# Weight transfers of 4 MB with 32 KB rows in a streamed mixture of experts, one Trainium2 core

## What is computed

```
gate_a, gate_b = ...                       # (256, 1024) each
mixed = sigmoid(gate_a) * (y_a @ moba_up) + sigmoid(gate_b) * (y_b @ hgrn_up)
x = x + mixed @ w_out
h2 = rmsnorm(x, norm2_w)
top_v, top_e = top_k(h2 @ router_w + router_b, 4);  top_w = softmax(top_v)
for each expert e:                         # 1024 x 2048 and 1024 x 1024 floats: 12 MB
    gu = h2[its tokens] @ w_gate_up[e] + b_gate_up[e]
    y = ((clip(up) + 1) * glu(gate)) @ w_down[e] + b_down[e]
x = x + sum of y * top_w;  out = rmsnorm(x, final_norm_w)
```

## Time and profile before

| | |
|---|---|
| time, median of 3 runs | 1134.95 us (1134.37 to 1135.22) |
| the profiled execution's own time | 1136.25 us |
| its span, first to last instruction | 1134.5 us |
| PE busy | 1059.2 us, 93% |
| DVE, ACT, POOL busy | 348.4, 222.7, 38.9 us |
| hardware queue of SP (q1) | 436.71 MB, 92.6% of 16 engines' span |
| TensorE clock granted | 0.999 |

### The profile page before, as it was taken

How to read it: one execution, slowest core, us unless ns; L and a number is a source line. 1 busy time by engine, 2 the same in 40 slices (tenths; PEclk the granted TensorE clock), 3 DMA queues, 4 the chain that set the end, 5 groups by cost and what they waited for, 6 DMA issues and landing times.

```text
span 1134.5 us, 13360 instructions
## 1 busy us (share of the span) xinstructions
PE 1059.2 (93%) x5613; PEld 519.9 (46%) x5613; DVE 348.4 (31%) x686; ACT 222.7 (20%) x354; POOL 38.9 (3%) x32
## 2 busy tenths in 40 slices
PE   7999999999999999999988888888888898899896
PEld 7889999734343443434333333333333334233332
DVE  4984788422303222222222222222112020303022
ACT  6645674201010101011010010101010101010002
POOL 0390000000000000000000000000000000000000
PEclk9999999999999999999999999999999999999999
DMA  9545669999999999999999999999999999999994
GB/s 320 190 150 215 231 215 365 368 415 415 430 428 428 426 430 427 428 428 427 429 426 428 427 428 428 428 429 426 429 428 428 428 426 428 428 427 427 428 425 201
DMA packets 47489, 439.17 MB, mean 387 GB/s; under 512 B 5388, under 2 KB 7848, under 8 KB 22600
## 3 DMA queue, kind: packets, MB, share of 16 engines
q1 hardware_dynamic: 45136, 436.71, 92.6%
q10 hardware_dynamic: 2296, 1.61, 0.5%
HBM read 437.26 MB, written 1.05 MB: 386 GB/s over the span
## 4 chain that ended last, share of the span: by engine, by line
PE 57%; DMA 41%; DVE 1%; issue 0%; ACT 0%; another core or an unknown queue 0%; DVEq 0%
DMA S<-in_w_gate_up_dram 21%; PE PS L1671 20%; DMA S<-in_w_down_dram 12%; PE PS L1730 9%; PE PS L1338 9%; DMA B<-in_w_gate_up_dram 4%; PE PS L1652 4%; DMA EXTRA<-in_w_gate_up_dram 4%; PE PS L1632 3%; PE PS L1351 1%; PE PS L1354 1%; PE PS L1357 1%; PE PS L1712 1%; PE PS L1692 1%; PE PS L1318 1%; PE PS L1389 1%
## 5 line engine op out<-in xcount | busy, mean ns | idle before, releaser
L1671 PE MATMUL PS<-S,M 128*64 128x512 f32 x1520 | 340.0, 596 | 28.5 <-DMA S<-in_w_gate_up_dram 22.0
L1671 PEld LDWEIGHTS PS<-S,M 128*64 128x64 f32 x1520 | 105.3, 137 | 241.9 <-issue 195.7
L1171 DVE TENSOR_SCALAR M<-PS 128x256 f32<-128x256 f32 x64 | 27.0, 423 | 531.8 <-PE PS L1671 531.8
L1730 PE MATMUL PS<-S,M 128*64 128x512 f32 x736 | 164.7, 595 | 17.1 <-DMA S<-in_w_down_dram 17.1
L765 ACT ACTIVATE M<-M 128x256 f32<-128x256 f32 x64 | 26.7, 417 | 495.4 <-DVE M L1171 495.4
L1730 PEld LDWEIGHTS PS<-S,M 128*64 128x64 f32 x736 | 52.0, 137 | 119.8 <-issue 102.5
L770 ACT COPY M<-PS 64x512 f32<-64x512 f32 x31 | 17.9, 578 | 276.4 <-PE PS L1730 276.4
L1185 DVE COPY M<-PS 128x512 f32<-128x512 f32 x32 | 22.1, 692 | 127.7 <-PE PS L1712 127.7
L1632 PE MATMUL PS<-M,X 128*128 128x128 f32 x480 | 59.0, 281 | 0.0
L1632 PEld LDWEIGHTS PS<-M,X 128*128 128x128 f32 x480 | 57.7, 196 | 0.0
L1652 PE MATMUL PS<-M,SELT 128*128 128x512 f32 x120 | 55.5, 605 | 0.0
(11 more groups left out here) (259 smaller groups left out, 978.3 us busy)
## 6 DMA issues: line engine op xcount, KB each, us to landing
S<-in_w_gate_up_dram SPq DMA_DIRECT2D x95, 2048.0 KB, 47.8
S<-in_w_down_dram SPq DMA_DIRECT2D x43, 2048.0 KB, 47.2
M<-in_w_gate_up_dram SPq DMA_DIRECT2D x12, 2048.0 KB, 46.5
EXTRA<-in_w_gate_up_dram SPq DMA_DIRECT2D x11, 2048.0 KB, 48.7
S<-in_w_in_dram SPq DMA_DIRECT2D x10, 2048.0 KB, 7.9
B<-in_w_gate_up_dram SPq DMA_DIRECT2D x10, 2048.0 KB, 48.5
B<-in_w_down_dram SPq DMA_DIRECT2D x7, 2048.0 KB, 48.2
EXTRA<-in_w_down_dram SPq DMA_DIRECT2D x6, 2048.0 KB, 48.0
```

Source lines behind the costliest of these rows:

```text
L1171: v.tensor_scalar(gate[:, c], g2[:, :, 0], LIMIT, None, ALU.min).then_inc(gate_ready, 1)
L1671: ins = mm(gu[half][64 * g:64 * g + 64, :], hTe[:, k, tok], gu_slot[slot][:, kk, c:c + 512], start=(k == 0), stop=(k == KD - 1))
L1730: ins = mm(dst[64 * n:64 * n + 64, :], actT[b][:, k, 64 * kh:64 * kh + 64], dn_slot[slot][:, k, 512 * n:512 * n + 512], start=(kh == 0 and ...
```

## The change

The rows of a transfer double. `wgu` has four input channels on a partition, `wdn` eight, so that a partition's share of a quarter of gate/up, or of a whole down matrix, is 32 KB in one piece. From the second pair on, two slices are one transfer of 4 MB (`load_unit`), issued when both slots are free. The exceptions are the whole first pair, the last pair's down weights, and the unit whose two slots would be slot 9 and slot 10, which do not touch (`by_slots`); these are 2 MB transfers of 16 KB rows as before. Over the run 80 transfers of 4 MB stand for 160 of 2 MB, and 32 slices stay as they were.

The 11 slots become one tensor W. For that the early buffers move: slot 0 holds a new buffer hi_d until late, and slice 0 of the first pair is now issued after hu3 and not before group "mu"; slices 8 and 9 take the early places of 9 and 10, and 10 that of 8.

The other order of channels asks for more. POOL regroups x within its rows (`regroup`), the router's weights are loaded in that order, the residual is added through a strided view, and `act_T` turns eight groups of 64 by 16 small matmuls in place of four transposes. The gates ga, gb and the units mu, hu are made by `split`, tokens by channels, and the mix is turned back by four units mT0 to mT3 of four 128x128 transposes each, which DVE and ACT split into mix_lo and mix_hi.

```diff
-        wgu = A["w_gate_up"].rearrange("l e (s p k) n -> (l e) s p (k n)", p=P, k=2)
-        wdn = A["w_down"].rearrange("l e (h p c) n -> (l e) h p (c n)", p=P, c=4)
+        wgu = A["w_gate_up"].rearrange("l e (u p k) n -> (l e) u p (k n)", p=P, k=4)
+        wdn = A["w_down"].rearrange("l e (p c) n -> (l e) p (c n)", p=P)
...
+        def by_slots(j, m, first_round):
+
+            return not first_round or ring(j, m) == 9 or j == 0 or j == PAIRS - 1 and m >= 8
...
             for n, what in enumerate(LOADS):
                 if what == GB1:
-                    load(0, 0, 9)
-                if what == "mu":
-                    filled(sp, "kT1")
-                    load(0, 0, 0)
+                    load(0, 0, 8)
                 if what == "wo0":
                     filled(sp, "ya1")
                     load(0, 0, 1)
                 if what == "wo1":
-                    load(0, 0, 10)
+                    sp.wait_ge(x_regrouped, 1)
+                    load(0, 0, 9)
                     sp.wait_ge(yb_ready, 1)
                     load(0, 0, 3)
...
             filled(sp, "hu3")
+            load(0, 0, 0)
             load(0, 0, 5)
-            sp.wait_ge(mix_ready, 1)
-            load(0, 0, 8)
+            filled(sp, "mT3")
+            load(0, 0, 10)
             filled(sp, "wo10")
...
-            def load_pair(p, e, j, stop=12):
-
-                for m in range(stop):
-                    used(p + (m - SLOTS) // 12, (m - SLOTS) % 12)
-                    load(e, j, m)
+            def load_pair(p, e, j, first_round, stop=12):
+
+                for m in range(0, stop, 2):
+                    if by_slots(j, m, first_round):
+                        for n in (m, m + 1):
+                            used(p + (n - SLOTS) // 12, (n - SLOTS) % 12)
+                            load(e, j, n)
+                    else:
+                        for n in (m, m + 1):
+                            used(p + (n - SLOTS) // 12, (n - SLOTS) % 12)
+                        load_unit(e, j, m)
...
+            pool.wait_ge(at_ready, 1)
+            pool.wait_ge(xn_ready, TT)
+            st.did(regroup(x_spare, X[:, 0, :]))
+            st.settle()
+            st.did(regroup(rows_of(1), X[:, 1, :]))
+            st.settle()
+            nc.gpsimd.tensor_copy(rows_of(0), x_spare).then_inc(x_regrouped, 1)
...
-                for c in range(4):
-                    ins = tr((gu[1] if b else multi)[:, P * c:P * c + P], act[:, P * c:P * c + P], ident)
+                if not isinstance(i, int):
+                    tr((gu[1] if b else multi)[:, 0:P], act[:, 0:P], ident)
+                for c in range(8):
+                    for g in range(2):
+                        rows, cols = slice(64 * g, 64 * g + 64), slice(64 * c, 64 * c + 64)
+                        ins = mm((gu[1] if b else multi)[rows, cols], act[rows, cols], ident[rows, rows],
+                                 start=True, stop=True)
                 ins.then_inc(actT_filled, 1)
...
-            split_T(*GATES[9])
+            split(*GATES[9])
             wait_drained(pe, "ya1")
+            def up(name, what, j, x_hi, x_lo, lo_there):
+                split(f"{name}{j}", what, j % 2, x_hi, x_lo, lo_there, kn=4, half=j // 2)
+
+            def turn_mix(j):
+
+                ps = begin(f"mT{j}")
+                pe.wait_ge(mix_step, j + 1)
+                for a in range(4):
+                    c = unit_cols(j).start + P * a
+                    ins = tr(ps[:, P * a:P * a + P], ga[:, c:c + P], ident)
+                end(ins)
```

More of the change, by code:

```diff
@@ L92 @@
             "pos0": 5, "pos1": 2, "all": 7, "wT": 6}
+OWN_BANK.update({"hu0": 2, "hu1": 3, "mT0": 4, "hu2": 5, "mT1": 2, "hu3": 3, "mT2": 6, "mT3": 7})
 UNITS = bank_units()
@@ L1053, in _, with mix, mixed_lo @@
                 lo("hu", j)
-            for j in range(4):
-                c = slice(512 * j, 512 * j + 512)
-                ve.wait_ge(sig_ready, 3)
+            def mix(j):
+                c = unit_cols(j)
                 filled(ve, f"hu{j}")
-                drain(f"hu{j}", v.tensor_tensor(gbT[:, c], bank(f"hu{j}")[:], gbT[:, c], ALU.mult))
-                st.settle()
-                st.did(v.tensor_tensor(flat[:, c], flat[:, c], gbT[:, c], ALU.add), mix_step)
-                if j < 2:
-                    lo("wo0", j)
-            st.settle()
-            st.did(v.tensor_scalar(SMALL[:, 609:610], eps, 1.0, None, ALU.mult), mix_ready)
+                drain(f"hu{j}", v.tensor_tensor(gb[:, c], bank(f"hu{j}")[:], gb[:, c], ALU.mult))
+                ve.wait_ge(drained_by["dve"], st.count[drained_by["dve"].name])
+                st.did(v.tensor_tensor(ga[:, c], ga[:, c], gb[:, c], ALU.add), mix_step)
+            def mixed_lo(j):
+                ve.wait_ge(mix_hi_ready, j + 1)
+                drain(f"mT{j}", v.tensor_tensor(mixed_chunk(mix_lo, j), turned_mix(j), mixed_chunk(mix_hi, j), ALU.subtract))
+            ve.wait_ge(sig_ready, 3)
+            mix(0)
+            lo("wo0", 0)
+            mix(1)
+            lo("wo0", 1)
+            mixed_lo(0)
+            mix(2)
+            mixed_lo(1)
+            mix(3)
+            mixed_lo(2)
+            mixed_lo(3)
             def residual(tt, n):
@@ L1338, in split_T, with split @@
                             ins = mm(ps[:, T * a:T * a + T], w[:, k, P * a:P * a + P], x[:, k, :],
-                                     start=(k == 0 and w is w_h and x is hi), stop=(k == kn - 1 and x is lo))
+                                     start=(k == 0 and w is w_h and x is hT_hi), stop=(k == KD - 1 and x is hT_lo))
                 end(ins)
-            def split(name, what, tt, hi=hT_hi, lo=hT_lo, lo_there=(hT_lo_ready, 1)):
+            def split(name, what, tt, hi=hT_hi, lo=hT_lo, lo_there=(hT_lo_ready, 1), kn=KD, half=0):
@@ L1348, in split @@
+                w_l = w_lo[s].rearrange("p (k n) -> p k n", k=kn)[:, :, 512 * half:512 * half + 512]
                 rows = slice(P * tt, P * tt + P)
-                pe.wait_ge(hi_ready, n + 1)
-                for k in range(KD):
-                    mm(ps[:].rearrange("p (j n) -> p j n", j=2), hi[:, k, rows], w_h[:, k], start=(k == 0), stop=False)
-                wait_lo(what, 1)
-                for k in range(KD):
-                    mm(ps[:], hi[:, k, rows], w_l[:, k, :], start=False, stop=False)
+                pe.wait_ge(hi_ready, last + 1)
@@ L1469, in _ @@
                     probs_T(h - 1)
-                split_T(*GATES[4 + h // 2])
+                split(*GATES[4 + h // 2])
             for j in range(2):
@@ L1476, in _ @@
             probs_T(7)
-            split_T(*GATES[8])
+            split(*GATES[8])
             wait_drained(pe, "pT7")
```

277 lines of the change are left out of this document (154 added, 123 removed).

## The result

The changed kernel takes **1137.89 us** in the median of 18 runs (1136.86 to 1140.78); the kernel before, on the same chips, 1135.39 (18 runs, 1134.37 to 1136.54). The ratio is **1.0024**, with a 95% interval of 1.0018 to 1.003: slower by 2.5 us. The forecast was 1133.5, with a range up to 1137.6. The profiled execution of the changed kernel took 1139.23 us with a span of 1137.4, so it is 1.3 us over its median.

The account below looks back on a forecast made before the run. The prediction took the full DMA stream plus PE's work after the last landing to bound the run. Start +1.0, transfers -4.3 and tail +1.8 gave -1.5 us, a median of 1133.5 us, range 1130.3 to 1137.6.

Parts of the forecast that it names:

- Part 1: Weight stream: 4 MB units with 32 KB rows save 54 ns each, 4.3 us over 80 units; ends 0 and 7.1 us.
- the choice of 6 ns: Weight stream: fixed DMA cost a packet, taken between nothing and the 10 ns derived from 16 KB and 2 KB rows.
- 36.8 ns "for a KB": Weight stream: size-dependent part of an engine's time for a row, from two equations on 16 KB and 2 KB rows.
- Part 2: Start of the stream, through pair 1: later slice 0 and two-slot waits make it 1.0 us later; ends -1 and +3.5.
- the holes: Opening, 210 to 230 us: DMA moved 356 and 357 GB/s; filling this would absorb 1 to 5 us of slice 0's 4.9.
- DVE and ACT lie under PE there: Opening, around the mix: DVE and ACT work stays hidden under PE, which gets 1.8 us earlier at the opening pair.
- Part 3: PE in a pair and at the end: dearer act_T hidden until the last pair; PE ends the run, 1.8 us later.
- 52.8 against 58.4: Each pair: PE time with the dearer act_T against DMA time, in us, so act_T is hidden until the last pair.
- so no clock is to be won: PE, whole run: the granted clock read 1.00, the higher of two levels, in both windows, so it could not improve.
- Rival (c): Opening, mix to pair 1: PE is late and the queue runs dry, +3.4 us, 1138.4; chance 0.12.
- (a): Weight stream: the larger row saves nothing or 3 ns, giving 1135.5 to 1137.8 us; chance 0.25.
- (b): Weight stream: the full 10 ns a packet hold, -7.1 + 2.8 = -4.3, giving 1130.7 us; chance 0.18.

Follow-up runs that it names:

- experiment 1: The changed kernel with every transfer at 2 MB, keeping the new layout, `act_T`, mix and slots: 1136.99 us, ratio 1.0012 to the kernel before.
- experiment 2: The changed kernel with pair 1 (the second pair) also in 2 MB transfers: 1135.04 us, ratio 0.9992 to the kernel before.
- experiment 7: The changed kernel with pair 1 in 2 MB transfers, each two issued one after the other when both slots are free: 1138.12 us, ratio 1.0023.
- experiment 5: The kernel before with ten more 64x64 matmuls in each `act_T`, their results overwritten: 1138.79 us, ratio 1.0025 to the kernel before.
- experiment 3: The changed kernel with the last pair wholly in 2 MB transfers: 1135.85 us, ratio 1.0 to the kernel before.
- experiment 10: The changed kernel with slices 2, 3, 6 and 7 of the last pair in 2 MB transfers: 1135.49 us.
- experiment 8: The changed kernel with slices 2 and 3 of the last pair in 2 MB transfers: 1138.65 us.
- experiment 9: The changed kernel with slices 6 and 7 of the last pair in 2 MB transfers: 1138.05 us.
- experiment 11: The changed kernel with three unused 512-column matmuls in PE's wait between slices 1 and 2 of the last pair: 1137.07 us.

## Where the prediction was right and where it failed

**The bound** was read rightly: the end is the end of the stream plus what follows. Every difference found lies in one of the three places it named: the start, the stream, the tail.

**Part 1, what a transfer costs, held.** 54 ns a unit were worked out, 58 measured by the medians and 70 by the landings, 4.3 us in all for 80 units against 4.6 (80 x 0.058) to 5.6. The choice of 6 ns in place of the 10 that the earlier trace rows gave was the right one, with luck in how near it is, since it was a choice between nothing and 10: 58 = 9 x f, eight rows and a report, makes 6.4 ns a packet (5 to 8), and 70 makes 7.8. (The 36.8 ns "for a KB" are for 1000 bytes, and of the fetches, which are 16 KB packets, four stand among the 2613 rows; neither changes the sum.) In the window from 300 to 400 us there are 1618 packets at 430 GB/s:

```profile
DMA packets 1618, 42.99 MB, mean 430 GB/s; under 512 B 176, under 2 KB 176, under 8 KB 176
```

Without the 176 small ones these are 1442 rows with 42.99 MB, which makes about 1180 of 32 KB and 260 of 16 KB (two slices of 2 MB), where the earlier trace rows had 2613 of 16 KB: a row of 32 KB isn't split. The estimate of 3.5 ns from the Trainium skill (DMA: Bandwidth & Descriptors, "Why small descriptors are slow", three cycles a packet) would make 28 ns a unit (8 x 3.5); the measurement is about twice that.

**Part 2 failed, and it is the main step that did.** It allowed 1.0 us for the start of the stream (slice 7 at 272.8, the outer end +3.5); slice 7 landed 4.7 us later than before (276.46 against 271.78), of which 2.85 us are seen in the median. Against the forecast its unit was issued 1.1 us later (261.43 for 260.3) and took 2.5 us longer to land (15.0 for 12.5). By bytes alone the forecast was 269.9 to 273.9, and experiments 1 and 2 are at 271.7: giving up the idle time for slice 0 was indeed paid for by the holes. What was wrong is the wait for two slots. I priced only the last unit of pair 1, at 12.5 us after its issue. All four issues, from the trace of the changed kernel:

```profile
L460 SPq DMA_DIRECT2D W<-in_w_gate_up_dram x4: 328/328/328, 230.6 to 261.4; - x4
...
DMA to landing us min/median/max: 12.5/14.8/15.0
```

Only the first takes 12.5, and it lands 0.5 us late, at 243.03. The next is issued at 240.78, with 2.25 us of work left in the queue; it lands at 255.41, 12.4 us after its forerunner where two slices would take 9.78. The next two come 11.0 and 10.05 us after theirs. The pauses of 0.5, 2.6, 1.2 and 0.3 us add up to nearly all of the 4.7, and of this only the 1.2 us at slice 9 (experiment 2) are made up. The forecast built on the shortest landing of 2 MB, 7.6 us, for a unit that stands behind three others with such a wait each. I had looked at the depth of the queue at one issue (10.2 us for slice 7, 4.9 of them its own transfer) and called it short, but had not asked at each issue of a unit how much was left, which was the forecast's own data: some 5.3 us of work stood ahead of slice 7, and a transfer that is issued one slice later finds a good part of that gone. Experiments 2 and 7 show the rest: same transfers, one wait or two, 1135.04 or 1138.12.

PE was also only 0.8 us earlier at the opening pair (219.96 against 220.76), not 1.8, which moved the last issue by a microsecond. The timelines show most of that: when the output projection begins, PE is 1.6 us ahead (185.18 against 186.79), with the last turning unit (0.35 us) still to come. "DVE and ACT lie under PE there" did not hold: PE waits 0.21 us for DVE before the third turning unit (184.79) and 0.41 us before the matmuls at 212.19; the kernel before shows no wait at either place.

**A term was missing:** that the longer program costs time in the stream. Part 3 called the dearer `act_T` hidden, "52.8 against 58.4", by PE's time alone. Its matmuls, 1024 where there were 128, and as many weight loads are also fetched, by the same DMA engines, and the prediction put that at nothing without a reason. Experiment 1 puts all of the change but the units at 1.4 us, and its trace has that in the stream, not in the opening or the tail; experiment 5 gets such a loss from the instructions alone, and in all three traces it is some 1.5 us for a round of eight fetches. The Trainium skill describes the fetch (Runtime: NRT & Kernel Launch, "Instruction fetch mechanics": code comes in blocks of 16 KB, and the cost of it is mostly hidden). The blocks agree with the rows, 0.61 MB in 37; that they are hidden does not hold here, where the DMA queue is the bound.

**Part 3, the tail, held, with one exception.** It said that slice 6 would be reached just when 6+7 is there, that PE and not the last landing would end the run, and that this costs 1.8 us. Experiments 3 and 10 give 2.0 and 2.4 for it, experiments 8 and 9 show that both units bind at once, and experiment 11, where the clock held, has 22.9 us from the landing of 6+7 (1102.13) to the end of the last `down`, forecast 22.7. The exception is "so no clock is to be won". There was some to be lost. Sum and rivals took PE's durations from full speed, and the new wait of 3.5 us in the last pair lets the clock fall to the lower level just where PE is the bound.

**The sum.** Forecast +1.0 - 4.3 + 1.8 = -1.5. Measured by the experiments: +2.85 (pair 1), +2.0 to 2.4 (last pair, the clock's share included), +1.4 (the longer program), -4.1 (the 71 other units): +2.2 to +2.6 against 2.5. The first two are net of the 9 units' own gain.

**The rivals.** Rival (c) ended nearest, 1138.4, and its sign in the profile appeared (a window under 420 between 230 and 300 us). That sign could not tell, though: the kernel before has such windows too, 410 from 230 to 240 and 395 from 270 to 280. And its mechanism was that PE would be late, and PE was early; the queue ran short by the way the units are issued. It had the right place and consequence and the wrong cause, and a chance of 0.12 was too small for a queue that was known to be short. Rivals (a) and (b), rows that save less or more, both fall.

## What to carry to other kernels

Ask of a larger transfer first not what it saves on the wire but how much is left in the queue at each moment when it could be issued: where the queue is short, at the start of a stream, keep the transfers small, and also before its last work, where a late landing leaves the compute engine to end the run (here 2 MB in the first two pairs and the last one, 4 MB between, 0.24% faster than before). Two late landings can hold the same end, so that undoing either alone shows nothing. And in a stage that DMA bounds, count the instructions that a change adds on an engine with time to spare, since their code comes through the same DMA engines (here 1.5 us for each eight fetches of 16 KB).

## What the runs showed of the hardware that was not expected

- TensorE's clock fell to its lower level (1.2 GHz) after PE had stood still for 3.5 us in the last pair, and sixteen matmuls took 5.35 and 6.53 us in two traces, 3.65 at full speed. In experiment 8 it fell after 2.65 us (5.17 us), in experiment 1 after 2.04 (5.35 us). It held after 2.04 us in the kernel before, 2.17 in experiment 7, 2.53 in experiment 5 and 0.62 in experiment 11: the length of the wait alone does not decide it.
- Seven and five more fetches of 16 KB of instructions went with 1.7 and 1.5 us lost in a stream of 830 us; their bytes alone are 0.3 and 0.2 us of 16 engines. In three traces the weights land late, by some 1.5 us in all, once for each eight fetches, behind the same one or two of the eight.
- A unit of 4 MB issued with 2.25 us left in the queue landed 2.6 us late, and halves of 2 MB issued at the same moment cost nearly the same (275.52 against 276.46 at slice 7).
